# Column norms, paired output slots, a third weight buffer and a compression block of its own in a 512-token network kernel

## The chip, the cores and the metric

The kernel runs on one core of a Trainium2 chip. The metric is device time in microseconds (us), lower is better. The engines are PE (TensorE: matmuls, with PEld for its weight loads), DVE (VectorE), ACT (ScalarE), POOL (GpSimd) and SP (SyncE, which here only issues loads and stores).

## The reference

Four blocks on one sequence of 512 tokens with 1024 features, all in f32: an even mixer (spatial gating and a causal convolution) with a convolutional FFN, an odd mixer (dilated attention) with a convolutional FFN, and then two layers of a second kind.

```python
def rms_norm(x, g):
    y = xf * lax.rsqrt(jnp.mean(xf * xf, axis=-1, keepdims=True) + EPS)
    return (y * g.astype(jnp.float32)).astype(x.dtype)

def layer_norm_2(x, g, b):
    ...
    return ((xf - mu) * lax.rsqrt(var + LN_EPS)).astype(x.dtype) * g + b

def conv_ffn(x, norm_g, w_up, conv_w, conv_b, w_down):
    h = rms_norm(x, norm_g)
    u = causal_dwconv(h @ w_up, conv_w, conv_b)
    gate, val = jnp.split(u, 2, axis=-1)
    return x + (jax.nn.silu(gate) * val) @ w_down

# first_block: for each of two layers
            x = x + jnp.concatenate([ya, yb], axis=-1) @ even_w_out[j]   # or x + o @ odd_w_o[j]
        x = conv_ffn(x, ...)
    return rms_norm(x, final_norm_g)

# second_block: for each of two layers
    proj = h @ w_in[l]
    mixed = jnp.concatenate([nsa_mixer(...), gla_mixer(...), pool_mixer(...)], axis=-1)
    h = layer_norm_2(DEEPNORM_ALPHA * h + mixed @ w_out[l], ln1_g[l], ln1_b[l])
    ff = jnp.square(jax.nn.relu(h @ w_up[l])) @ w_down[l]
    h = layer_norm_2(DEEPNORM_ALPHA * h + ff, ln2_g[l], ln2_b[l])

# inside nsa_mixer, for keys and for values
        hid = jax.nn.gelu(tb.reshape(B, G, n_cmp, CMP_BLOCK * Dh) @ w1)
        return hid @ w2
```

Each norm needs, for every token, one or two sums over 1024 features, and its result is the input of the next product.

## The kernel before

Activations lie with features on the 128 partitions and the 512 tokens along them, in DC = 8 chunks of 128 features (`X`, `HH`, `HL`). All weights come as one stream of 376 slots of 128 x 1024 (512 KB each). SP loads slot s into `RAW[:, s % 2]`; ACT rounds it into `WH` (`split_hi`), DVE makes the remainder `WL` (`split_lo`), and a product is three passes, WH x HH, WH x HL and WL x HH, so one slot is 24 matmuls of 512 columns. There are two buffers, so `split_hi` of slot s waits until the matmuls of slot s-2 are over (`tile_done`), and the load into RAW waits for the `split_lo` of slot s-2.

A slot is used in one of two ways. `project` makes one output tile of 128 features from all eight chunks of the input. `add_rows` takes one chunk of the input and adds to all eight output chunks, in eight PSUM banks; on the last slot of such a product it reports each output chunk (`y_done`), and DVE's `add_out` adds it to X and reports `x_ready`. The first tile after a norm (`first_tiles`) goes chunk by chunk behind ACT and DVE, which make HH (`h_hi`) and HL (`h_lo`).

There are seven RMS norms (named even, v, conv, f0, odd, f1, final; v and conv are halves with a mean of their own) and four layer norms (ln1_0, ln2_0, ln1_1, ln2_1, the last of which ends the program). In every one, the sum over features is a matmul of a 128 x 128 matrix of ones with a chunk of squares (`sum_squares`, L1118, or `sum_rows`, L1109, for the mean), which leaves the sum in all 128 partitions. ACT takes the root of a full 128 x 512 tile (`root`, L571) and DVE its reciprocal (`spread`, L1658). For f0, odd and f1 the norm is applied after the projection, so the chain root, reciprocal runs beside tile 1, and `sum_squares` is interleaved in the first tile. For `final` and the layer norms nothing of the next product can start before it. There, to spare PE, DVE adds the last chunks up first (`squares_part`, and L1979 into MU), so that PE sums five chunks and one partial sum. A layer norm then runs: sums of X (L1109, L1113), `mean` (L1639), `centre` (L1653, x8), squares on ACT (L560), their sums (L1118), root, reciprocal, rows (L1990) with HH (L816) and HL (L1994).

The NSA compression has for keys and for values one hidden product of 64 small matmuls (64 x 128 by 31 columns, alternating between the two halves of the array). `hidden` (L1375) returns a function that `project` calls after each chunk, so they stand interleaved in tiles 5 and 7 of `mix_layer`. Its weights W1 (2 MB) and four smaller arrays are loaded by POOL (L517), once a layer, when the last slot before the layer is over (`tile_done` at `L_IN[l]`). PE first reads one of them at L1349, in tile 3, behind a wait for all five.

## Time and profile before

| | |
|---|---|
| median of three runs | 2591.74 us (2590.53 to 2593.21) |
| the profiled execution | 2597.57 us, of which its span is 2595.8 us |
| PE busy | 2463.1 us, 95% of the span |
| DVE busy, ACT busy | 1417.6 us (55%), 1087.1 us (42%) |
| POOL busy | 51.7 us (2%) |
| DMA | 210.38 MB, mean 81 GB/s |

The times of the trace are those of the profiled execution, which is 5.8 us above the median. "Idle before" a row is the time in which its engine stood still ahead of it, with the engine and line that ended the wait. The granted clock is TensorE's, 1.00 being its full level of 2.4 GHz and 0.50 the lower one of 1.2 GHz. A matmul's duration counts from its start to its last result, so a run of back-to-back matmuls is better read by the distance of their starts. In the trace one f32 matmul of the program is two PE instructions, and one of fp32r is one.

### The profile page before, as it was taken

Reading aid. Unit: us, or ns where it says so; the run is one execution under the profiler, and the core shown is the slowest. Engines: PE = TensorE matmul, PEld = TensorE weight load, DVE = VectorE, ACT = ScalarE, POOL = GpSimd, SP = SyncE. Lnnn points to the kernel's source line nnn. Section 1 sums busy time; section 2 is a strip of 40 time slices with the busy share of each in tenths; the row PEclk is TensorE's granted clock in tenths of the full one; section 3 lists DMA queues with packets and bytes.
Section 4 is the critical chain, followed back from the end, with each engine's and each line's share of the span. In section 5 each row is a group of like instructions: output and inputs, shape, how many; then the busy total and the mean of one; then the engine's idle time right before and its main releaser. Section 6 shows DMA issues by size and latency. Waiting matters only on the chain.

```text
span 2595.8 us, 33416 instructions
## 1 busy us (share of the span) xinstructions
PE 2463.1 (95%) x11814; PEld 1938.8 (75%) x11814; DVE 1417.6 (55%) x2298; ACT 1087.1 (42%) x1649; POOL 51.7 (2%) x64
## 2 busy tenths in 40 slices
PE   8989999998998999999988989999989889899997
PEld 6667888877777788886766668888857666688885
DVE  5876777236763777724367664244263774532434
ACT  4534444237883544413445443223154543431322
POOL 0000000000000000000011000000000210000000
PEclk9999999999999999999999999999999989999999
DMA  4212333321222233333211113333322112233331
GB/s 170 62 45 89 95 95 95 97 88 57 65 65 68 87 97 97 94 97 113 66 49 41 43 63 97 97 97 97 97 86 66 33 33 81 65 97 97 95 97 68
DMA packets 57422, 210.38 MB, mean 81 GB/s; under 512 B 6478, under 2 KB 6880, under 8 KB 56960
## 3 DMA queue, kind: packets, MB, share of 16 engines
q1 hardware_dynamic: 56736, 204.51, 25.7%
q0 software_dynamic: 608, 4.81, 0.5%
q8 instruction: 52, 0.85, 0.1%
q14 instruction: 26, 0.21, 0.0%
HBM read 207.20 MB, written 2.10 MB: 81 GB/s over the span
## 4 chain that ended last, share of the span: by engine, by line
PE 82%; DVE 8%; ACT 7%; issue 2%; DVEq 1%; DMA 0%; SPq 0%; ACTq 0%
PE PS L1081 14%; PE PS L1083 14%; PE PS L1082 14%; PE PS L1097 10%; PE PS L1099 10%; PE PS L1098 10%; PE PS L1118 2%; ACT PT L720 1%; PE PS L1256 1%; ACT RT L732 1%; ACT PB L714 1%; DVE RSTD L1658 1%; DVE PB L1886 1%; DVE WL L1635 1%; PE PS L1109 1%
## 5 line engine op out<-in xcount | busy, mean ns | idle before, releaser
L1635 DVE TENSOR_TENSOR WL<-RAW,WH 128x1024 fp32r<-128x1024 f32 x376 | 462.4, 1230 | 650.4 <-ACT WH L555 649.8
L555 ACT ACTIVATE WH<-RAW 128x1024 fp32r<-128x1024 f32 x376 | 397.5, 1057 | 819.4 <-PE PS L1099 560.9
L1081 PE MATMUL PS<-HH,WH 128*128 128x512 f32 x1792 | 713.3, 398 | 2.0 <-DVE WL L1635 1.9
L1083 PE MATMUL PS<-HH,WL 128*128 128x512 f32 x1792 | 699.6, 390 | 0.0
L1082 PE MATMUL PS<-HL,WH 128*128 128x512 f32 x1792 | 699.4, 390 | 0.0
L1081 PEld LDWEIGHTS PS<-HH,WH 128*128 128x128 f32 x1792 | 338.0, 189 | 77.8 <-issue 6.9
L1083 PEld LDWEIGHTS PS<-HH,WL 128*128 128x128 f32 x1792 | 337.4, 188 | 71.3
L1082 PEld LDWEIGHTS PS<-HL,WH 128*128 128x128 f32 x1792 | 338.0, 189 | 70.4 <-issue 3.4
L1099 PE MATMUL PS<-MH,WL 128*128 (+1 forms) x864 | 336.1, 389 | 0.0
L1097 PE MATMUL PS<-MH,WH 128*128 (+1 forms) x864 | 336.1, 389 | 0.0
L1098 PE MATMUL PS<-ML,WH 128*128 (+1 forms) x864 | 336.1, 389 | 0.0
L1097 PEld LDWEIGHTS PS<-MH,WH 128*128 128x128 f32 x864 | 162.2, 188 | 33.7
L1098 PEld LDWEIGHTS PS<-ML,WH 128*128 128x128 f32 x864 | 162.2, 188 | 33.6
L1099 PEld LDWEIGHTS PS<-MH,WL 128*128 128x128 f32 x864 | 162.2, 188 | 33.6
L1818 DVE SCALAR_TENSOR_TENSOR NBF<-NBF,VEC 128x511 f32<-128x511 f32 (+1 forms) x176 | 131.6, 748 | 14.1 <-issue 13.5
L2274 DVE TENSOR_TENSOR SB<-RB 128x512 f32<-128x512 f32 x64 | 44.3, 692 | 166.9 <-ACT RB L1055 166.9
L1055 ACT ACTIVATE RB<-PS 128x512 f32<-128x512 f32 x64 | 38.3, 598 | 209.4 <-PE PS L1083 203.2
L714 ACT ACTIVATE PB<-PB,NEGMAX 128x512 f32<-128x512 f32 (+3 forms) x160 | 87.7, 550 | 44.0 <-DVE NEGMAX L1873 44.0
L1811 DVE TENSOR_TENSOR NBF<-PS,RSTD 128x512 f32<-128x512 f32 x88 | 60.9, 692 | 80.1 <-PE PS L1083 79.9
L1134 PE MATMUL PS<-HH,WH 128*128 128x512 f32 x96 | 51.1, 532 | 37.6 <-DVE HL L1994 21.0
L1097 PE MATMUL PS<-HH,WH 128*128 128x512 f32 x192 | 76.6, 399 | 3.1 <-DVE HL L2182 3.1
L1873 DVE CUSTOM_DVE_ANT_0 PB<-PS,TAB 128x512 f32<-128x512 f32 (+3 forms) x160 | 68.5, 486 | 19.3 <-issue 19.3
(273 smaller groups left out, 2568.6 us busy)
## 6 DMA issues: line engine op xcount, KB each, us to landing
RAW<-wstream SPq DMA_DIRECT2D x376, 512.0 KB, 3.6
W<-cmp_w POOLq DMA_DIRECT2D x2, 2048.0 KB, 8.8
X<-xt SPq DMA_DIRECT2D x4, 512.0 KB, 6.8
out<-X SPq DMA_DIRECT2D x8, 256.0 KB, 2.0
TAB<-tables SPq DMA_DIRECT2D x1, 1871.5 KB, 12.9
WS<-spatial_w SPq DMA_DIRECT2D x1, 512.0 KB, 8.7
BS<-spatial_b SPq DMA_DIRECT2D x1, 256.0 KB, 9.2
PW<-pool_w POOLq DMA_DIRECT2D x2, 128.0 KB, 2.4
```

The lines of the kernel that those rows point to most:

```text
L555: act.activation(WH[:, b, :], RAW[:, b, :], ACT.Copy).then_inc(w_hi, 1)
L714: act.activation(row, row, ACT.Exp, scale=-1.0, bias=NEGMAX[:, 4 * e + i:4 * e + i + 1], accum_out=SUM[:, 4 * e + i:4 * e + i + 1]).then_i ...
L1081: pe.matmul(PS[:, bank, :], WH[:, b, w], HH[:, k, :], start=(k == 0), stop=False)
L1082: pe.matmul(PS[:, bank, :], WH[:, b, w], HL[:, k, :], start=False, stop=False)
L1083: last = pe.matmul(PS[:, bank, :], WL[:, b, w], HH[:, k, :], start=False, stop=(k == DC - 1))
L1097: pe.matmul(PS[:, n, :], WH[:, b, w], rh, start=first, stop=False)
L1098: pe.matmul(PS[:, n, :], WH[:, b, w], rl, start=False, stop=False)
L1099: last = pe.matmul(PS[:, n, :], WL[:, b, w], rh, start=False, stop=final)
L1635: dve.tensor_tensor(WL[:, b, :], RAW[:, b, :], WH[:, b, :].bitcast(F32), ALU.subtract).then_inc(w_lo, 1)
L1811: dve.tensor_tensor(ZF[:, b, :], PS[:, b, :], RSTD[:], ALU.mult).then_inc(f_z, 1)
L1818: ins = dve.scalar_tensor_tensor(acc, ZF[:, b, 0:T - back], w[:, 2 - back:3 - back], acc, ALU.mult, ALU.add)
L1873: dve.tensor_tensor_reduce(PB[:, e, row], head_banks(e)[:, row], tab(mask)[:, T - w:T], 1.0, 3.0e38, ALU.add, ALU.min, NEGMAX[:, 4 * e + i ...
```

## The change

It has six parts.

1. **Pairs.** Ahead of each of the eight norms that follow an `add_rows` product (f0, odd, f1, final, and the four layer norms) the last two slots are taken together (`add_pair`): output chunk by output chunk, six matmuls each, instead of one slot after the other. It waits for the `w_lo` of both slots. For `final` and the layer norms the sums of output chunk n-3 (`LAG`) stand inside the pair, behind chunk n.
2. **Column sums.** `sum_tokens` takes the data as the 128 x 128 weights and a single column of ones as the moving side, four matmuls a chunk (one per 128 tokens), which leaves the 512 sums as a 128 x 4 block, tokens on partitions. Root and reciprocal work on [128, 4]. `widen` brings them back to 128 x 512: four matmuls with the column spread over 128 columns as weights and the identity as the moving side, into a PSUM bank. DVE reads that bank directly, or, for even, f0, odd and f1, copies it to RSTD first (`keep_rstd`). The layer norm's mean goes the same way, so it has two widens. DVE's partial sums are gone. Only conv keeps the old form.
3. **Third weight buffer.** The slot of the next first tile is split into `WX` (`early_hi`, `early_lo`), which is free throughout the last slots before the norm. `first_tiles` runs WH x HH, WL x HH and only then waits for `h_lo` for WH x HL.
4. **Compression block.** `hidden` is a block of 64 matmuls of its own behind tile 5 and tile 7.
5. **POOL's loads** wait for `L_IN[l] + 1` finished slots, that is, also for the first tile of the layer.
6. **Smaller things.** The squares of f0, f1 and final have a buffer SQF of their own. In f0 `fill_scaled` writes HH rows 6 and 7, which E_OUT's pair reads, only when the pair is over. In odd the root stands behind `raw_k` on ACT as before, but the PE's widen, inside tile 1, now waits for it.

```diff
             def squares(buf, src, order, ready, base):
...
-                act.activation(STD[:], PS[:, bank, :], ACT.Sqrt, scale=1.0 / width, bias=eps).then_inc(n_std, 1)
+                if nm == "conv":
+                    act.activation(STD[:], PS[:, bank, :], ACT.Sqrt, scale=1.0 / width, bias=eps).then_inc(n_std, 1)
+                else:
+                    act.activation(COL[:, COL_STD:COL_STD + TT], PS[:, bank, 0:TT], ACT.Sqrt, scale=1.0 / width, bias=eps)\
+                       .then_inc(n_std, 1)
...
-                pool.wait_ge(tile_done, L_IN[l])
+                pool.wait_ge(tile_done, L_IN[l] + 1)
...
+            def early_hi(s):
+
+                act.wait_ge(w_loaded[0], 16 * (s // 2 + 1))
+                if s:
+                    act.wait_ge(tile_done, s - 2)
+                act.activation(WX[:, 0, :], RAW[:, 0, :], ACT.Copy).then_inc(w_hi, 1)
...
                 pe.wait_ge(w_lo, 2 * i + c + 1)
                 for k in range(DC):
+                    if beside and k == beside[0]:
+                        widen(*beside[1:])
...
-                    if beside:
-                        beside(k)
...
+            def add_pair(i, rows, beside=None):
+
+                pe.wait_ge(w_lo, 2 * i + 2)
+                for n in range(DC):
+                    w = slice(n * P, (n + 1) * P)
+                    for b, (rh, rl) in enumerate(rows):
+                        pe.matmul(PS[:, n, :], WH[:, b, w], rh, start=False, stop=False)
+                        pe.matmul(PS[:, n, :], WH[:, b, w], rl, start=False, stop=False)
+                        last = pe.matmul(PS[:, n, :], WL[:, b, w], rh, start=False, stop=(b == 1))
+                        if n == DC - 1:
+                            last.then_inc(tile_done, 1)
+                        elif b:
+                            last.then_inc(y_done, 1)
+                    if beside and n >= LAG:
+                        beside(n - LAG)
...
+            def sum_tokens(buf, n, bank, final):
+
+                for t in range(TT):
+                    last = pe.matmul(PS[:, bank, t:t + 1], buf[:, n, t * P:(t + 1) * P], tab("ones")[:, 0:1],
+                                     start=(n == 0 and t == 0), stop=(final and t == TT - 1))
+                return last
+
+            def widen(nm, col, bank):
+
+                pe.wait_ge(n_col, WIDE[nm])
+                for t in range(TT):
+                    last = pe.matmul(PS[:, bank, t * P:(t + 1) * P], COL[:, col + t:col + t + 1].to_broadcast([P, P]),
+                                     tab("identity"), start=True, stop=True)
+                last.then_inc(n_wide, 1)
...
-                        pe.wait_ge(h_lo, fill + k + 1)
-                        pe.matmul(PS[:, b, :], WH[:, b, w], HH[:, k, :], start=(k == 0), stop=False)
-                        pe.matmul(PS[:, b, :], WH[:, b, w], HL[:, k, :], start=False, stop=False)
-                        last = pe.matmul(PS[:, b, :], WL[:, b, w], HH[:, k, :], start=False, stop=(k == DC - 1))
+                        wh, wl = first_weights(b, w)
+                        pe.wait_ge(h_hi, fill + k + 1)
+                        pe.matmul(PS[:, b, :], wh, HH[:, k, :], start=(k == 0), stop=False)
+                        pe.matmul(PS[:, b, :], wl, HH[:, k, :], start=False, stop=False)
+                        pe.wait_ge(h_lo, fill + k + 1)
+                        last = pe.matmul(PS[:, b, :], wh, HL[:, k, :], start=False, stop=(k == DC - 1))
...
-            project(base, 1)
+            project(base, 1, beside=(1, "odd", COL_RSTD, 3))
...
             def layer_norm(nm):
-                sum_rows(X, 0, [(n, x_ready, XR[nm] + n + 1) for n in range(FIRST)], n_add, (n_part, PART[nm] + 1))
-                for n in range(FIRST):
-                    sum_squares(NB2, n, 3, nm, False)
-                sum_squares(NB2, FIRST, 3, nm, True, (n_part, PART[nm] + 2))
+                for n in range(DC - LAG, DC):
+                    last = sum_ready(nm, n)
+                last.then_inc(n_add, 1)
+                widen("mean_" + nm, COL_MEAN, 1)
+                for n in range(DC):
+                    sum_squares(NB2, n, 2, nm, n == DC - 1)
+                widen(nm, COL_RSTD, 3)
...
-                tile(5, hidden(0))
+                tile(5)
+                hidden(0)
...
             split_lo(base, 1)
+            inverse_root("odd")
             split_lo(base, 2)
-            spread("odd")
+            keep_rstd("odd")
```

On PE, around the first layer norm (ln1_0), the program of before has, from the last three matmuls of the product to the first of the next tile (X is the residual, NB2 the squares, TAB holds the ones):

```order
L1097 MATMUL PS<-HH,WH 128x512
L1098 MATMUL PS<-HL,WH 128x512
L1099 MATMUL PS<-HH,WL 128x512
L1109 MATMUL PS<-X,TAB 128x512 [waits x_ready] x5
L1113 MATMUL PS<-MU,TAB 128x512 [waits n_part]
L1118 MATMUL PS<-NB2,TAB 128x512 [waits n_sq] x5
L1118 MATMUL PS<-NB2,TAB 128x512 [waits n_part]
L1134 MATMUL PS<-HH,WH 128x512 [waits h_lo,w_lo]
```

The same place after the change, from the fifth token sum inside the pair on; the last two sums of X and seven of the eight chunks of squares, which read like their neighbours, are left out, and COL is the 128 x 4 block:

```order
L1144 MATMUL PS<-HH,WH 128x512
L1145 MATMUL PS<-HL,WH 128x512
L1146 MATMUL PS<-HH,WL 128x512
L1165 MATMUL PS<-TAB,X 128x1 [waits x_ready]
L1165 MATMUL PS<-TAB,X 128x1 x3
...
L1173 MATMUL PS<-TAB,COL 128x128 [waits n_col]
L1173 MATMUL PS<-TAB,COL 128x128 x3
L1165 MATMUL PS<-TAB,NB2 128x1 [waits n_sq]
L1165 MATMUL PS<-TAB,NB2 128x1 x3
...
L1203 MATMUL PS<-HH,WX 128x512 [waits h_hi,w_lo]
```

Five of eight sums of X moved ahead of the product's end; six matmuls of the squares became thirty-two of one column; two groups of four are new, each behind a wait for DVE.

On DVE, at the same norm, before:

```order
L1689 SCALAR_TENSOR_TENSOR X<-X,PS 128x512 [waits tile_done]
L1979 TENSOR_TENSOR MU<-X 128x512 [waits x_ready]
L1979 TENSOR_TENSOR MU<-MU,X 128x512 [waits x_ready]
L1635 TENSOR_TENSOR WL<-RAW,WH 128x1024 [waits w_hi]
L1639 TENSOR_SCALAR MU<-PS 128x512 [waits n_add]
L1653 TENSOR_TENSOR X<-X,MU 128x512 x8
L1646 TENSOR_TENSOR NB2<-NB2 128x512 [waits n_sq] x2
L1658 RECIPROCAL RSTD<-STD 128x512 [waits n_std]
L1990 SCALAR_TENSOR_TENSOR NB2<-X,VEC,RSTD 128x512 x2
```

and after (L1721 and L1635 are the same `split_lo`, L1777 and L1689 the same addition, L2082 and L1990 the same row):

```order
L1777 SCALAR_TENSOR_TENSOR X<-X,PS 128x512 [waits tile_done]
L2072 TENSOR_SCALAR COL<-PS 128x4 [waits n_add]
L1721 TENSOR_TENSOR WL<-RAW,WH 128x1024 [waits w_hi]
L1735 TENSOR_TENSOR X<-X,PS 128x512 [waits n_wide]
L1735 TENSOR_TENSOR X<-X,PS 128x512 x7
L1740 RECIPROCAL COL<-COL 128x4 [waits n_std]
L2082 SCALAR_TENSOR_TENSOR NB2<-X,VEC,PS 128x512 [waits n_wide]
L2082 SCALAR_TENSOR_TENSOR NB2<-X,VEC,PS 128x512
```

Four full-width additions are gone, the mean and the reciprocal shrank from 128 x 512 to 128 x 4, and `split_lo` moved behind the mean.

On PE, in tile 5 of `mix_layer` (TB the keys' blocks, W1 the compression weights), before, one chunk of eight:

```order
L1375 MATMUL PS<-TB,W1 64x31 x8
L1081 MATMUL PS<-HH,WH 128x512
L1082 MATMUL PS<-HL,WH 128x512
L1083 MATMUL PS<-HH,WL 128x512
L1375 MATMUL PS<-TB,W1 64x31 x8
```

and after, from the end of tile 5 to the start of tile 6:

```order
L1117 MATMUL PS<-HH,WH 128x512
L1118 MATMUL PS<-HL,WH 128x512
L1119 MATMUL PS<-HH,WL 128x512
L1453 MATMUL PS<-TB,W1 64x31 [waits c_tb]
L1453 MATMUL PS<-TB,W1 64x31 x63
L1117 MATMUL PS<-HH,WH 128x512 [waits w_lo,z_kept]
```

The eight groups of eight stand in one row.

## Rows read from the trace of the kernel before

**Rows 1.** The page, part 1: busy time, share of the span, instructions of each engine.
```profile
PE 2463.1 (95%) x11814; PEld 1938.8 (75%) x11814; DVE 1417.6 (55%) x2298; ACT 1087.1 (42%) x1649; POOL 51.7 (2%) x64
```

**Rows 2.** The page, part 4: the chain that ended last, by engine.
```profile
PE 82%; DVE 8%; ACT 7%; issue 2%; DVEq 1%; DMA 0%; SPq 0%; ACTq 0%
```

**Rows 3.** Timeline, last two slots ahead of ln1_0: start, us, what.
```profile
1504.53 0.39 PE L1097 MATMUL PS<-HH,WH 128*128 128x512 f32 x1
1504.76 0.39 PE L1098 MATMUL PS<-HL,WH 128*128 128x512 f32 x1
...
1505.88 1.23 DVE L1635 TENSOR_TENSOR WL<-RAW,WH 128x1024 fp32r<-128x1024 f32 x1 [4.21 <-ACT WH L555]
```

**Rows 4.** Timeline, ln1_0 from the product's end to the first tile.
```profile
1515.42 4.46 PE L1109 MATMUL PS<-X,TAB 128*128 128x512 f32 x10
...
1518.05 0.20 ACT L565 ACTIVATE WARM<-TAB 128x1 f32<-128x1 f32 x1
...
1521.54 4.91 DVE L1653 TENSOR_TENSOR X<-X,MU 128x512 f32<-128x512 f32 x8
...
1522.94 4.56 PE L1118 MATMUL PS<-NB,TAB 128*128 128x512 f32 x10 [2.21 <-ACT NB L560]
...
1529.94 3.35 DVE L1658 RECIPROCAL RSTD<-STD 128x512 f32<-128x512 f32 x1 [1.94 <-ACT STD L571]
1533.38 1.42 DVE L1990 SCALAR_TENSOR_TENSOR NB<-X,VEC,RSTD 128x512 f32<-128x512 f32 x2
...
1535.82 0.77 PE L1134 MATMUL PS<-HH,WH 128*128 128x512 f32 x1 [6.64 <-DVE HL L1994]
```

**Rows 5.** Timeline: matmuls with 128 x 128 weights and 31 moving columns.
```profile
1293.83 0.31 PE L1392 MATMUL PS<-HID,W 128*128 128x31 f32 x2
1294.07 0.40 PE L1393 MATMUL PS<-W,HID 128*31 128x128 f32 x2
```

**Rows 6.** Timeline: matmuls with 64-row weights, alternating between the array's halves.
```profile
1359.11 1.08 PE L1401 MATMUL PS<-KCS,ZT 64*128 64x31 f32 x16
1361.82 0.80 PE L1424 MATMUL PS<-ZS 64*128 64x512 f32 x2 [1.62 <-DVE ZT L2132]
```

**Rows 7.** Windows: stretch, length, busy time of PE, PEld, DVE, ACT, POOL, then granted clock.
```profile
1520.70:1522.90 2.20, 0.03 (x1) 0.00 (x0) 2.06 (x4) 0.64 (x2) 0.00 (x0) 1.00 0.68 223
...
1532.20:1535.80 3.60, 0.00 (x0) 0.01 (x1) 3.38 (x5) 1.63 (x3) 0.00 (x0) 0.50 0.00 0
...
1361.00:1364.00 3.00, 2.18 (x10) 1.82 (x11) 2.16 (x6) 0.41 (x1) 1.64 (x3) 0.57 0.00 0
```

**Rows 8.** Waits by line: us in total, times, longest (tile 2 behind even, f0, f1).
```profile
PE PS L1081 <- DVE WL L1635: 1.9, 3, 0.7
```

**Rows 9.** Timeline, odd: the keys' copies on ACT and the first scores on PE.
```profile
598.29 0.63 ACT L756 ACTIVATE KS<-KR 64x512 fp32r<-64x512 f32 x1 [0.61 <-DVE KR L1897]
...
604.13 1.54 PE L1272 MATMUL PS<-KL,QS 64*128 64x512 f32 x8 [5.14 <-DVE QS L1909]
```

**Rows 10.** Timeline, final: sums of squares and the first tile.
```profile
1212.02 5.31 PE L1118 MATMUL PS<-NBF,TAB 128*128 128x512 f32 x12
...
1223.82 0.76 PE L1134 MATMUL PS<-HH,WH 128*128 128x512 f32 x1 [6.48 <-DVE HL L1672]
```

**Rows 11.** Timeline, tile 5 of layer 0: two of the eight interleaved groups.
```profile
1259.29 0.65 PE L1375 MATMUL PS<-TB,W 64*64 64x31 f32 x16
...
1260.77 0.65 PE L1375 MATMUL PS<-TB,W 64*64 64x31 f32 x16
```

**Rows 12.** The page, part 6: POOL's 2 MB load, KB each, us to landing.
```profile
W<-cmp_w POOLq DMA_DIRECT2D x2, 2048.0 KB, 8.8
```

**Rows 13.** Timeline, layer 0: POOL's first and last load, PE's first use.
```profile
1212.85 0.75 POOL L517 DMA_DIRECT2D GW<-gate_w  x1 [1196.91 <-PE PS L1099]
...
1215.20 0.54 POOL L517 DMA_DIRECT2D W<-cmp_w  x1
...
1243.09 1.56 PE L1349 MATMUL PS<-GW,ZT 17*128 17x192 f32 x8
```

242 lines of the change are left out of this document (142 added, 100 removed).

## The prediction

> **What bounds the kernel now.** I read the busy times first, then the chain that ended last, then the timeline around each norm. PE is busy for 95% of the span [rows 1] and carries 82% of the chain [rows 2]: a plain slot is 24 matmuls 0.226 us apart [rows 3], 5.44 us, and all else hides beside it. What is left for other engines, 15% for DVE and ACT [rows 2], lies where PE has nothing to multiply. At a layer norm that is the stretch from the product's end at 1515.42 to the first tile at 1535.82, 20.40 us [rows 4], of which PE sums for 4.46, then 4.56, and waits 2.21 and 6.64 us, with the 3.35 us reciprocal as the longest single step. So the norms are worth attacking; the question is what the replacement costs on PE, which is the bound. All sums are against the profiled execution (2597.57 us, 5.8 above the median); I add them to the median.
>
> **The pair's wait.** `add_pair` waits for both slots' weights. The second one's split can't begin before slot s-3 is over, since there are two buffers. The trace has this order of events: the slot starts at 1504.53, ACT rounds, DVE's remainder starts at 1505.88 and ends 1.23 later, at 1507.11 [rows 3]. Before, that was hidden by the slot then running. Now nothing else is ready: PE stands for 1507.11 - 1504.53 = 2.6 us, at eight places. Behind it on PE is only the pair; but everything after it shifts. It buys little: the output chunks appear 1.36 us apart instead of 0.68, so DVE's adds no longer fall behind and the sums of the early chunks can be made inside, yet the last chunk comes at the same end. WX lets the next slot's split go on meanwhile, off the path.
>
> **The price of one token sum.** One chunk was one f32 matmul of 512 columns: ten PE instructions take 4.46, so 0.86 us for two [rows 4]. It becomes four matmuls, eight instructions, each with its own 128 x 128 weights and one moving column. No such instruction is in the trace. From above: two instructions with 128 x 128 weights and 31 columns take 0.24 us up to the next line [rows 5], 0.12 each with the change of line. From below: sixteen with 64-row weights, alternating between the halves of the array, take 1.08 to the last result; a lone one lasts 0.20 (0.31 less 0.11, [rows 5]), so they start (1.08 - 0.20) / 15 = 0.06 apart [rows 6]. I take 0.11, because the token sums fill all 128 rows with one weight block after another, as in rows 5. Then a chunk costs 8 x 0.11 = 0.88, no less than before; between other matmuls I count 1.0, for the changes of kind. The narrow side doesn't pay: it saves columns, and the loads of weights take their place. The loads themselves overlap in rows 6 since halves alternate. A rule of the Trainium skill fits this (page "TensorE: Matmul & The Clock Gate", section "The mechanism": a weight load overlaps running matmuls only when its row group differs), and the two rows agree with it, 0.11 against 0.06. Another rule of the same page speaks for less (section "Back-to-back issue gap": matmuls of 1 to 64 columns at about 60 cycles, or an issue floor near 25 ns); by it the kernel would come out faster, near the second rival's time.
>
> **A layer norm, step by step** (ln1_0, in the times of before). Pair over, with five token groups inside: 1515.42 + 2.6 + 5 x 1.0 = 1523.0. Three groups left: 1525.6. Mean on [128, 4], priced like the 0.20 us ACT step on one column [rows 4]: 1525.9. Then DVE makes `split_lo`, 1.23, which hides the 0.9 us widen: centring starts at 1527.1, against 1521.54 [rows 4], 5.6 later. Before, it was the other way: that split ran under the sums. The first square is there 1.4 after centring starts (1522.94 - 1521.54 [rows 4]): 1528.5. Eight groups on PE, 7.0, are slower than ACT's squares (0.6 each), so 1535.5. Root and reciprocal 0.2 each with 0.25 of hand-over: 1536.15. Widen with its hand-over 1.0: rows at 1537.15, against 1533.38 [rows 4]: 3.8 later. So the reciprocal's 3.2 us are won, and 2.6 of waiting, two widens and unshared sums cost more. The first tile gets back 0.4, as one matmul instead of three stands behind the last HL. Per norm 3.4, and 3.8 for the last, which has no tile: **+14.0** with TensorE at its full clock.
>
> **The clock.** From the end of the pair (1523.0) to the first tile (some 1539) PE has nothing but one-column sums and a widen. The rows show the following: after 2.2 us of no work the clock is still 1.00 [rows 7]; after the sums of squares end and PE stands, it is 0.50 from 1532.2 on [rows 7]. And at 1359.11 sixteen narrow matmuls run, then PE is idle for 1.62 us only [rows 6], and still the clock falls in that stretch (0.57 on the mean of 1361 to 1364 [rows 7]). Had narrow matmuls held the clock up, an idle time shorter than 2.2 should not have lowered it. So I take it that one-column sums don't count as work and the squares run at the lower level, 1.2 GHz. At half rate the eight groups cost another 7.0 and the widen 0.9: +7.9 each, **+31.6** for four. The wait inside the pair (2.6) is near the 2.2 that didn't lower it; up to 0.9 at each of eight, counted for the range alone.
>
> **The RMS norms.** f0 and f1: 2.6 for the pair, 1.0 for the widen inside tile 1; root and reciprocal are ready by then. Sums cost as before. The idle 0.6 or so ahead of tile 2 [rows 8] goes, because the 3.35 reciprocal no longer holds up DVE's split: +3.0 each. even: the widen 1.0, less that idle 0.7, and 1.0 for v's, less 0.2 of sums: +1.1. In v the reciprocal was hidden by tap matmuls. odd: 2.6; PE's widen waits about 3 us in tile 1, since the root stands behind `raw_k` on ACT, but PE has 5.14 idle later [rows 9], waiting for the scores' operands. Tile 1 ends later, ACT's work on the queries too, and its copies of the keys start 1.1 after the 598.29 of before [rows 9]; less 0.4 in the first tile: +3.3. final: 1212.02 [rows 10] + 2.6 + 5.0 + 2.6 for sums, 0.65, 1.0: rows at 1223.9 against 1221.5 (2.3 ahead of the first tile, as in rows 4 and 10); less 0.4: +1.9. Its first tile was at half clock and stays so. Together **+12.3**.
>
> **POOL's loads.** Issued after tile 0 instead of before it: 1212.85 before [rows 13]; tile 0 starts at 1223.82 [rows 10] and, part of it at half clock, ends near 1233.9. The 2 MB load is the fifth on the queue, 2.35 behind the first [rows 13], and takes 8.8 [rows 12]: 1233.9 + 0.3 + 2.35 + 8.8 = 1245.4, against 1243.09 for the first use [rows 13]. RAW's 512 KB loads share the engines now: 2.3 to 3.4 late, 3.0 taken, twice: **+6.0**. Before, it was over long in advance.
>
> **The compression block.** Two groups are 1.48 us apart [rows 11], of which 3 x 0.226 = 0.68 is the tile's: 0.80 a group, 6.4 for eight. Sixteen start (0.65 - 0.20) / 15 = 0.03 apart [rows 11]; 128 in a row take 4.0 with both ends. That is 2.35 saved, four times: **-9.4**. ACT and DVE are not late there, so it goes through in full.
>
> **Sum.** 14.0 + 31.6 + 12.3 + 6.0 - 9.4 = +54.5: 2591.74 + 54.5 = 2646.2; with a little for the waits' clock, 2648.
>
> **Rival 1, the clock holds.** Same prices, but one-column sums (which do keep PE's queue and its weight loads busy) count as work: 54.5 - 31.6 = +22.9, 2614.6; with the waits' clock up to 2620. For it: through the interleaved narrow groups of rows 11 the clock stays up. Against: full matmuls stand between those.
>
> **Rival 2, the other side: the token sums are cheap.** If a block of weights goes in while the other one is in use, as in rows 6, an instruction is 0.06, a chunk 0.5 alone and 0.62 in between. A layer norm then has its mean at 1515.42 + 2.6 + 3.1 + 1.5 + 0.2 = 1522.8, centres at 1524.1 to 1524.5, its sums keep pace with ACT's squares, and the rows start at 1532.2: 1.1 earlier, and 0.4 of the first tile, -5.8 for four. The RMS norms come to +0.8 instead of 12.3, loads and block stay: -8.4, **2583.3**. It decides at the price per instruction: between 0.11 (+22.9) and 0.06 (-8.4) zero lies near 0.075. With the clock down in the squares it is a gain of 1 or nothing.
>
> **Rival 3: pairs or loads don't cost what I say.** If POOL's loads are in time, -6; the pairs' waits are structural, and without them alone all would be 21 less. Neither changes the sign of the forecast; they sit in the range.
>
> **How the numbers follow.** Forecast (full weight loads, low clock) 0.57, 2640 to 2662. Rival 1 0.26, 2608 to 2622. Rival 2 0.17: 2583 in 0.11, no change in 0.06. The likeliest gives 2648. Leaving out rival 2 leaves out 0.17, so the range is 2608 to 2662. Slower 0.83, within 0.2% (5 us, about what a measurement of this kernel can tell from no change) 0.06, faster 0.11.
>
> **What would show it.** In the profile after: an idle of 2.6 us ahead of each pair, ended by DVE's WL; token instructions 0.11 apart at full clock and 0.22 in the squares of the layer norms, with a granted clock of 0.50 there; 18 us from centring to rows of a layer norm (10 with the clock up) where 11.8 were [rows 4]; at L1349's counterpart an idle of 3 us ended by POOL's load; 4.0 us for the compression block. Wrong if the instructions stand 0.06 apart, or the clock stays at 1.00 through the squares.

## The result and the profile after

The changed kernel takes 2673.3 us (median of four runs, 2665.98 to 2685.01) against 2592.47 for the kernel before: 1.0317 times as long, interval 1.0281 to 1.0353, or 81 us more. The forecast was slower, 2648, with a range to 2662. The direction was right, the size was not. One run of the small-loads kernel below took 3231.33 us at a mean granted clock of 0.734 and is left out of that kernel's median. The profiled run of after is one of the two faster ones, 2665.98 us with a span of 2664.2; against the profiled run of before it is 68.4 longer.

The page of after, parts 1 and 4, to be read beside [rows 1, 2]. PE is busier by 71 us, although it does no more full matmuls, and the token sums (L1165) are the largest new line of the chain.

```profile
PE 2534.0 (95%) x12610; PEld 2058.9 (77%) x12610; DVE 1377.4 (52%) x2284; ACT 1083.0 (41%) x1649; POOL 51.8 (2%) x64
...
PE 83%; DVE 7%; ACT 6%; issue 2%; DMA 1%; DVEq 1%; POOL 0%; SPq 0%; ACTq 0%; POOLq 0%
```

The waits of PE in after: total us, times, longest. The first and the last of these lines don't exist in before; they are the pairs and POOL's loads.

```profile
PE PS L1144 <- DVE WL L1721: 20.4, 8, 2.6
...
PE PS L1429 <- DMA W<-cmp_w: 6.4, 2, 3.5
```

The timeline of after at ln1_0, which answers to [rows 3, 4] (L1144 is the pair, L1165 a token sum, L1173 a widen, L1735 centring, L2082 the row, L1203 the first tile):

```profile
1527.40 0.47 PE L1144 MATMUL PS<-HH,WH 128*128 128x512 f32 x1 [2.56 <-DVE WL L1721]
...
1543.66 3.63 PE L1165 MATMUL PS<-TAB,X 128*128 128x1 f32 x32
...
1547.54 1.16 PE L1173 MATMUL PS<-TAB,COL 128*128 128x128 f32 x8 [0.25 <-DVE COL L2072]
1548.74 4.87 DVE L1735 TENSOR_TENSOR X<-X,PS 128x512 f32<-128x512 f32 x8
...
1550.14 13.81 PE L1165 MATMUL PS<-TAB,NB 128*128 128x1 f32 x64 [1.44 <-ACT NB L579]
1563.99 0.26 ACT L593 ACTIVATE COL<-PS,TAB 128x4 f32<-128x4 f32 x1 [9.72 <-PE PS L1165]
1564.29 0.18 DVE L1740 RECIPROCAL COL<-COL 128x4 f32<-128x4 f32 x1 [10.68 <-ACT COL L593]
1564.52 2.08 PE L1173 MATMUL PS<-TAB,COL 128*128 128x128 f32 x8 [0.57 <-DVE COL L1740]
1566.63 1.40 DVE L2082 SCALAR_TENSOR_TENSOR NB<-X,VEC,PS 128x512 f32<-128x512 f32 x2 [2.17 <-PE PS L1173]
...
1568.28 0.76 PE L1203 MATMUL PS<-HH,WX 128*128 128x512 f32 x1 [1.68 <-ACT HH L843]
```

The wait stands ahead of the pair as predicted. Thirty-two token instructions take 3.63 us, 0.11 each; sixty-four take 13.81, 0.22 each. From centring to the first row it is 17.9 us, where before had 11.8 and the prediction said 18. The reciprocal has shrunk from 3.35 to 0.18. The windows of after around the same norm (length, busy times, then the granted clock):

```profile
1528.50:1532.00 3.50, 3.50 (x10) 2.70 (x9) 0.86 (x2) 0.00 (x0) 0.00 (x0) 0.52 0.81 274
1532.00:1546.00 14.00, 14.00 (x90) 12.50 (x88) 4.63 (x7) 2.06 (x2) 0.00 (x0) 1.00 0.01 4
...
1549.50:1568.00 18.50, 15.89 (x72) 15.51 (x72) 5.65 (x10) 5.62 (x10) 0.00 (x0) 0.50 0.09 29
```

The lowest line is the forecast's stretch at half clock. The highest was not in the sum: 1.2 us after the pair's wait of 2.56 the clock falls to half for some 3.4 us, in the middle of full matmuls. Such a stretch stands at six of the eight pairs, all but those of f0 and ln2_1; it begins between 0.3 us before PE resumes (ln2_0) and 1.2 us after it (ln1_0).

Where the 68.4 us of the two profiled runs lie, by the start of the same slots in both:

| stretch | forecast | measured |
|---|---|---|
| even block, into E_OUT | +1.1 | +2.2 |
| f0: pair, first tile, tile 1 | +3.0 | +4.2 |
| odd: the same | +3.3 | +4.2 |
| odd attention | 0 | +2.5 |
| f1: pair, first tile, tile 1 | +3.0 | +7.3 |
| final: pair to first tile | +1.9 | +3.7 |
| mixer of layer 0, of layer 1 (loads, block) | -1.7, -1.7 | -3.9, -1.6 |
| ln1_0, ln2_0, ln1_1 | +11.3 each | +12.6, +13.2, +12.7 |
| ln2_1, to the end | +11.7 | +11.4 |
| sum | +54.5 | +68.4 |

At each of the eight pairs PE starts 2.7 us later than it would without the wait, 2.6 of waiting and 0.1 of restart.

The lower clock can be added up in the same way. In the profiled run of before TensorE is at half level for 105 us of the span, in that of after for 211. Of the 106 us more, 82 lie in the four layer norms, counted from the pair to the end of the first tile or tiles, and 24 in all other places together. Where PE is busy throughout, a microsecond at half level costs half a microsecond.

### The profile page after: what moved, and what is told of

Its sections match the earlier page's. It is cut to its first block, busy times and chain, and to the rows that moved or that the text cites. A ratio compares the mean times of both kernels' runs of the same rounds, so it can differ in the third digit from the quotient of the medians.

```text
span 2664.2 us, 34958 instructions
## 1 busy us (share of the span) xinstructions
PE 2534.0 (95%) x12610; PEld 2058.9 (77%) x12610; DVE 1377.4 (52%) x2284; ACT 1083.0 (41%) x1649; POOL 51.8 (2%) x64
## 4 chain that ended last, share of the span: by engine, by line
PE 83%; DVE 7%; ACT 6%; issue 2%; DMA 1%; DVEq 1%; POOL 0%; SPq 0%; ACTq 0%; POOLq 0%
PE PS L1117 13%; PE PS L1119 13%; PE PS L1118 13%; PE PS L1131 8%; PE PS L1133 8%; PE PS L1132 8%; PE PS L1165 4%; PE PS L1144 1%; ACT PB L740 1%; PE PS L1328 1%; ACT RT L758 1%; ACT PT L746 1%; PE PS L1146 1%; PE PS L1145 1%; DVE WL L1721 1%
## 5 line engine op out<-in xcount | busy, mean ns | idle before, releaser
L1721 DVE TENSOR_TENSOR WL<-RAW,WH 128x1024 fp32r<-128x1024 f32 x368 | 452.5, 1230 | 608.0 <-ACT WH L567 607.6
L1117 PE MATMUL PS<-HH,WH 128*128 128x512 f32 x1792 | 710.4, 396 | 0.0
L1131 PE MATMUL PS<-MH,WH 128*128 (+1 forms) x800 | 311.2, 389 | 0.0
L1132 PE MATMUL PS<-ML,WH 128*128 (+1 forms) x800 | 311.2, 389 | 0.0
L1133 PE MATMUL PS<-MH,WL 128*128 (+1 forms) x800 | 311.2, 389 | 0.0
L1131 PEld LDWEIGHTS PS<-MH,WH 128*128 128x128 f32 x800 | 150.2, 188 | 31.3
L1133 PEld LDWEIGHTS PS<-MH,WL 128*128 128x128 f32 x800 | 150.2, 188 | 31.1
L1132 PEld LDWEIGHTS PS<-ML,WH 128*128 128x128 f32 x800 | 150.2, 188 | 31.1
L702 ACT ACTIVATE NBF<-NBF,VEC 128x512 f32<-128x512 f32 x88 | 70.4, 800 | 6.8 <-DVE NBF L1906 6.8
L1165 PEld LDWEIGHTS PS<-TAB,NB 128*128 128x128 f32 x352 | 67.2, 295 | 7.4 <-ACT NB L579 6.6
## 6 DMA issues: line engine op xcount, KB each, us to landing
TAB<-tables SPq DMA_DIRECT2D x1, 1871.5 KB, 13.2
```

Source lines behind the costliest of these rows:

```text
L702: act.activation(ACCS[:, b, :], ZF[:, b, :], ACT.Identity, scale=w[:, 2:3], bias=w[:, 3:4]).then_inc(f_acc, 1)
L1117: pe.matmul(PS[:, bank, :], WH[:, b, w], HH[:, k, :], start=(k == 0), stop=False)
L1131: pe.matmul(PS[:, n, :], WH[:, b, w], rh, start=first, stop=False)
L1132: pe.matmul(PS[:, n, :], WH[:, b, w], rl, start=False, stop=False)
L1133: last = pe.matmul(PS[:, n, :], WL[:, b, w], rh, start=False, stop=final)
L1165: last = pe.matmul(PS[:, bank, t:t + 1], buf[:, n, t * P:(t + 1) * P], tab("ones")[:, 0:1], start=(n == 0 and t == 0), stop=(final and t = ...
```

## The experiments

Every run has the kernel before beside it on the same chip, at 2593.0 to 2595.2 us.

### The compression block alone

```diff
-                tile(5, hidden(0))
+                tile(5)
+                hidden(0)
```
(and the same for tile 7, on the kernel before)

> The kernel before with one edit, the compression block: the hidden products stand as one block behind tiles 5 and 7 instead of interleaved in them. Theory: 128 instructions start 0.03 us apart in a row and the 0.3 us per group for the changes of kind goes, 2.35 us at each of four places: -9.4, 2583 us. Rival (the interleaved matmuls cost nothing, since they wait on the same weights and PE is held by ACT and DVE in those tiles): 0, 2592 us.

Measured: 2584.87 us, ratio 0.9966 (0.9954 to 0.9977): -8.3. The theory holds. By slots, each tile behind a block starts 2.3 earlier, relative to the kernel before, as forecast (2.35); the median shows 8.3 of the 9.4.

### The pairs undone

```diff
             def add_pair(i, rows, beside=None):

-                pe.wait_ge(w_lo, 2 * i + 2)
-                for n in range(DC):
-                    w = slice(n * P, (n + 1) * P)
-                    for b, (rh, rl) in enumerate(rows):
+                for b, (rh, rl) in enumerate(rows):
+                    pe.wait_ge(w_lo, 2 * i + b + 1)
+                    for n in range(DC):
+                        w = slice(n * P, (n + 1) * P)
...
-                    if beside and n >= LAG:
-                        beside(n - LAG)
+                        if b and beside and n >= LAG:
+                            beside(n - LAG)
```

> The changed kernel with the pairs undone: the last two slots run one after the other, each behind the wait for its own weights; the sums inside stay in the last slot. Theory: the wait of 2.6 us goes at eight places (-21.8 with the restart), and with it the stretches at half clock that the trace shows 1 to 3 us behind a wait at several of them (1.7 us each): 2637 to 2650 us. Rival (the wait alone, no clock): -21.8, 2651 us. Second rival (the wait only moves to the next slot, because the sums inside then wait for DVE's additions, which come 0.68 us apart): 0 to -8, 2665 to 2673 us.

Measured: 2649.65 us (2637.81 to 2658.89), ratio to before 1.0212 (1.019 to 1.0235), 23.7 less than the changed kernel. The wait has gone from PE's list, and nothing took its place: the wait of the token sums for ACT (5.8 us in all) is the same with and without pairs. The second rival is out. Between the first two, the wait alone (-21.8) and the wait with its clock (down to -36), the median doesn't decide. The trace does. From pair to first tile, over all eight norms, this kernel's profiled run is 24.1 us shorter than after's, against 21.8 for the waits. It has no short half-clock stretch behind the start of the last two slots any more, but at ln1_0 the clock now falls earlier in the norm, during the sums of X, and the first widen pays for it as well:

```profile
1532.03 4.37 PE L1165 MATMUL PS<-TAB,X 128*128 128x1 f32 x32
1536.66 2.07 PE L1173 MATMUL PS<-TAB,COL 128*128 128x128 f32 x8 [0.26 <-DVE COL L2072]
```

```profile
1517.50:1534.60 17.10, 17.10 (x105) 15.15 (x103) 7.84 (x10) 4.30 (x4) 0.00 (x0) 1.00 0.22 67
1534.80:1562.00 27.20, 23.25 (x97) 21.46 (x98) 11.54 (x19) 9.69 (x18) 0.00 (x0) 0.50 0.06 20
```

In after these two rows are 3.63 and 1.16. The time at half level around ln1_0 is 27.3 us in both kernels (3.4 + 23.9 in after), and over all eight norms 137 us here against 139. Without the wait the norms get back the wait and little else: the first rival fits the trace best.

### The pairs' wait filled

```diff
+                for _ in range(11):
+                    pe.matmul(PS[0:128, DC - 1, :], ZERO[:], rows[0][0], start=False, stop=False)
                 pe.wait_ge(w_lo, 2 * i + 2)
```

> The changed kernel with eleven matmuls of a block of zeros, 512 columns each (2.5 us), put ahead of each pair's wait. They add zero to a bank, so nothing else changes; the wait is only filled. Theory (the idle wait lowers the clock and the pair pays for it, 1.7 us at five to eight places): -8 to -14, 2659 to 2665 us, and a granted clock of 1.00 through all pairs. Rival (a wait of 2.6 us costs only itself): 0, 2673 us.

Measured: 2665.51 us (2651.89 to 2678.55), ratio to before 1.0293 (1.0272 to 1.0314); 7.8 less than the changed kernel, with 11 more matmuls at eight places. In the trace of this run, ahead of ln1_0's pair:

```profile
1517.21 2.74 PE L1142 MATMUL PS<-HH,ZERO 128*128 128x512 f32 x11
1519.84 0.50 PE L1147 MATMUL PS<-HH,WH 128*128 128x512 f32 x1
```

and its windows over the filling and over the first part of the pair:

```profile
1517.00:1519.80 2.80, 2.80 (x13) 2.05 (x11) 1.24 (x2) 2.01 (x2) 0.00 (x0) 1.00 0.13 51
1519.80:1524.00 4.20, 4.20 (x19) 3.45 (x19) 2.50 (x3) 0.00 (x0) 0.00 (x0) 1.00 0.58 179
```

Where after has 0.52, this has 1.00, at the same place of the program and with the pair starting as late; the same holds at all eight pairs. So it is the idle time that lowers the clock there. But what this saves is small, because the clock then falls earlier in the norm behind it:

```profile
1519.80:1538.20 18.40, 18.36 (x113) 16.23 (x112) 6.63 (x9) 2.54 (x3) 0.00 (x0) 1.00 0.18 58
1538.40:1565.50 27.10, 23.39 (x93) 21.15 (x94) 13.08 (x21) 11.37 (x20) 0.00 (x0) 0.50 0.07 20
```

The eight stretches from pair to first tile are 4.5 us shorter than in after, 3.3 of it at f1 alone; the other 9.6 us between the two profiled runs lie in places that the edit doesn't touch. The medians' -7.8 is at the near end of what was expected, but the two kernels' runs overlap (2651.89 to 2678.55 against 2665.98 to 2685.01). The expected clock at the pairs is shown; the expected price of 1.7 us at each of them is not.

### Full matmuls among the token sums

```diff
             def layer_norm(nm):
...
+                busy(2)
                 widen("mean_" + nm, COL_MEAN, 1)
+                busy(8)
                 for n in range(DC):
+                    busy(2)
                     sum_squares(NB2, n, 2, nm, n == DC - 1)
```
(`busy(k)`: k matmuls of 512 columns into a free bank, on the changed kernel)

> The changed kernel with full matmuls of 512 columns, whose results nobody reads, put into the four layer norms: two ahead of the mean's widen, eight behind it and two ahead of each chunk's squares sums. They cost PE 0.45 us a chunk. Theory (one-column sums don't count as work, so the clock falls; the full ones hold it up): a chunk's sums go from 1.72 to 0.88 us at a granted clock of 1.00, so that with the filling a chunk takes 1.4 to 1.5, the widens 0.9 instead of 2.1, and the first tile runs at full clock: -3 to -4 per norm, -14 in all, 2659 us. Rival (the squares' sums cost 1.72 whatever the clock is): +3.6 for each norm's filling, +14, 2687 us.

Measured: 2688.2 us (2676.22 to 2694.05), ratio to before 1.0362 (1.034 to 1.0385), 14.9 more than the changed kernel. That is the number of the rival, but by luck: the timeline of ln1_0 in this run shows neither of the two:

```profile
1560.03 0.95 PE L1165 MATMUL PS<-TAB,NB 128*128 128x1 f32 x8
1560.84 0.72 PE L1400 MATMUL PS<-HH 128*128 128x512 f32 x2
1561.39 0.95 PE L1165 MATMUL PS<-TAB,NB 128*128 128x1 f32 x8
...
1564.13 0.98 PE L1165 MATMUL PS<-TAB,NB 128*128 128x1 f32 x8
...
1565.97 1.70 PE L1165 MATMUL PS<-TAB,NB 128*128 128x1 f32 x8
1567.53 1.20 PE L1400 MATMUL PS<-HH 128*128 128x512 f32 x2
1568.53 1.70 PE L1165 MATMUL PS<-TAB,NB 128*128 128x1 f32 x8
```

with the windows before and behind the change:

```profile
1560.00:1564.80 4.80, 4.80 (x38) 4.48 (x37) 2.82 (x5) 3.48 (x6) 0.00 (x0) 1.00 0.15 60
1565.00:1575.40 10.40, 10.35 (x41) 9.50 (x41) 0.00 (x0) 0.01 (x1) 0.00 (x0) 0.50 0.00 0
```

For four chunks the clock is 1.00 and a group of sums takes 0.95 to its last result, 1.36 to the next group with the filling in between; for the other four it is 0.50, 1.70 and 2.56. So the same instructions cost half as much when the clock is up, as the theory says, but this filling did not hold the clock up to the end of the sums. PE was busy almost without a gap in both windows. What failed was the means, not the price: every filling matmul ran at 0.42 us instead of 0.24 from then on.

### The layer norms' squares through the matrix of ones

```diff
             def sum_squares(buf, n, bank, nm, final):
...
-                if nm == "conv":
+                if nm == "conv" or nm.startswith("ln"):
                     last = pe.matmul(PS[:, bank, :], tab("ones"), buf[:, n, :], start=(n == 0), stop=final)
...
-                widen(nm, COL_RSTD, 3)
...
-                inverse_root(nm)
-                dve.wait_ge(n_wide, WIDE[nm])
+                dve.wait_ge(n_std, NORM[nm][1] + 1)
+                dve.reciprocal(RSTD[:], STD[:])
+                dve.drain()
```
(and the root and the rows on full tiles)

> The changed kernel with one thing undone in the four layer norms: the sums of squares go through the matrix of ones again, 512 columns, all eight chunks, with the root and the reciprocal on full tiles. The mean stays in columns, the pairs stay. Theory (one-column sums run at half clock, 1.72 us a chunk against 0.86 for the ones, and cost more than the narrow reciprocal saves): from the start of centring to the first row 12.8 us instead of 17.9, -5.1 at four places, -20, 2653 us; a little more if the first tile is at full clock too. Rival (at equal clock, 0.88 a chunk, the narrow form would be 2 to 3 us shorter than this one, so that undoing it costs): +8 to +12, 2681 to 2685 us.

Measured: 2659.95 us (2653.09 to 2668.03), ratio to before 1.026 (1.024 to 1.028): -13.4. The sign is the theory's, against the rival: even with the 3.35 us reciprocal back, the wide form is shorter here, at the clock that each form gets; the two at equal clock were not compared. The size is less than the 20 expected, and the timeline shows why (L1181 are the ones):

```profile
1554.63 4.87 DVE L1734 TENSOR_TENSOR X<-X,PS 128x512 f32<-128x512 f32 x8
...
1556.04 9.92 PE L1181 MATMUL PS<-NB,TAB 128*128 128x512 f32 x16 [1.44 <-ACT NB L579]
```

Sixteen instructions should take 6.9 (0.43 each, [rows 4]). They take 9.92, because the clock is already down when they start, behind the mean in columns:

```profile
1556.00:1562.00 6.00, 5.96 (x8) 2.59 (x9) 3.50 (x6) 4.16 (x7) 0.00 (x0) 0.53 0.21 81
1562.00:1566.00 4.00, 3.96 (x10) 1.45 (x8) 0.00 (x0) 0.00 (x1) 0.00 (x0) 1.00 0.00 0
```

Three us a norm, at most 12 in all: what follows a narrow stretch pays for it.

### POOL's small loads early

```diff
-                pool.wait_ge(tile_done, L_IN[l] + 1)
-                for dst, src in ((GW, gate_w), (PW, pool_w), (W2, cmp_w2), (CP, cmp_p), (W1, cmp_w1)):
+                pool.wait_ge(tile_done, L_IN[l])
+                for dst, src in ((GW, gate_w), (PW, pool_w), (W2, cmp_w2), (CP, cmp_p)):
                     pool.dma_start(dst[:], src[l]).then_inc(m_loaded, 16)
+                pool.wait_ge(tile_done, L_IN[l] + 1)
+                pool.dma_start(W1[:], cmp_w1[l]).then_inc(w1_loaded, 16)
```
(and DVE waits for `w1_loaded` ahead of the compression blocks)

> The changed kernel with the four small loads of POOL issued where they were before, at the end of the last slot before a layer, and the 2 MB load alone left behind the first tile, with a semaphore of its own that DVE waits for ahead of the compression blocks. Theory (PE's first use, which waited for all five loads, needs a small one only): the idle of 3.5 and 2.8 us in tile 3 goes, and with it the stretch at half clock that follows it in both layers (about 2 each): -6 to -10, 2663 to 2667 us. Rival (the 2 MB load is needed soon after anyway, by the compression blocks, and the wait only moves there): 0, 2673 us.

Measured: 2664.63 us (median of five, 2655.46 to 2676.33), ratio to before 1.0288 (1.0268 to 1.0308): -8.7, within the expected 6 to 10, though the runs overlap with after's. In the trace the two mixers are 4.4 and 4.6 us shorter than in after, against waits of 3.5 and 2.8. The wait is gone (L1432 is after's L1429; there it stood idle for 3.54):

```profile
1266.72 0.60 PE L1428 MATMUL PS<-TAB,ZT 128*128 128x128 f32 x4
1267.24 1.56 PE L1432 MATMUL PS<-GW,ZT 17*128 17x192 f32 x8
```

W1 can't go first as well: its memory is the third weight buffer's, which the first tile reads. That is where the later load comes from.

### Three parts undone at once, and then the mean

The first kernel of this section is the three edits above together (pairs, ones for squares, small loads). The second has in addition:

```diff
-                return sum_tokens(X, n, 0, n == DC - 1)
+                return pe.matmul(PS[:, 0, :], tab("ones"), X[:, n, :], start=(n == 0), stop=(n == DC - 1))
...
-                widen("mean_" + nm, COL_MEAN, 1)
...
+                if slot:
+                    split_lo(0, slot)
                 dve.wait_ge(n_add, ADD[nm])
-                dve.tensor_scalar(COL[:, COL_MEAN:COL_MEAN + TT], PS[:, 0, 0:TT], 1.0 / D, None, ALU.mult).then_inc(n_col, 1)
-                if slot:
-                    split_lo(0, slot)
-                dve.wait_ge(n_wide, WIDE["mean_" + nm])
-                centre(X, range(DC), PS[:, 1, :])
+                dve.tensor_scalar(MU[:], PS[:, 0, :], 1.0 / D, None, ALU.mult)
+                dve.drain()
+                centre(X, range(DC))
```

> The changed kernel with three parts undone at once: the pairs, the column sums of squares of the layer norms (ones again, as in the run for that alone) and the four small loads of POOL. What is left of the change is the column form in the other norms, the mean in columns, the third weight buffer, the order in the first tile and the compression block. Theory, parts that add up: 2673.3 less 23.7 (pairs, measured), less 20 (ones), less 6 to 10 (loads) = 2620 to 2624 us. From the kernel before upwards the steps alone give less: 2593 - 8.3 for the block, + 12 for the mean in columns (3 at each layer norm), + 4 for eight full sums instead of six, + 3 for the widens of the other norms = 2604 us. The gap between the two is what the clock costs in the narrow stretches that are left; if the clock did not matter there, the run should be near 2604.

Measured: 2632.91 us (2618.72 to 2638.59), ratio 1.0146 (1.0122 to 1.0169), 40.4 less than the changed kernel. The three alone gave 23.7 + 13.4 + 8.7 = 45.8: they add up to within the spread of the runs. It misses the 2620 to 2624 that was expected, and is 29 above the 2604 that steps at full clock would give.

> The run with three parts undone (pairs, column squares of the layer norms, small loads; 2632.9 us), and now the layer norms' mean too goes through the matrix of ones, with the full-width mean on DVE and its split ahead of it as before. What is left of the change: the column form in the RMS norms and v, the third weight buffer, the order in the first tile, the compression block, and eight full sums where two partial ones were shared with DVE. Theory (the mean in columns delays centring by 4.3 us a norm, for the token groups inside the last slot, the widen and DVE's split in between, and its narrow stretch lowers the clock, so that the ones sums behind it take 9.4 instead of 6.9): -6.7 at four places, 2606 us. Rival (only the delay, while the clock falls there in any case): -4.3 at four places, 2616 us.

Measured: 2627.04 us (2614.65 to 2631.47), ratio 1.0133 (1.0115 to 1.0151), only 5.9 less by the medians. The two profiled runs, 2629.67 and 2614.65, are 15 apart, and by slots each of the first three layer norms costs 3.6 more than in before, where it cost 6.7 with the mean in columns. So the mean in columns is 3.1 a norm in the traces; of the clock's share in it the medians say nothing certain. At ln1_0, the time at half level goes from 17.1 to 10.2 us. Neither expectation is met in its number.

What is left is mostly the RMS norms and v: by the first tile of the second half this kernel's profiled run is 12.0 behind before, with no pair in it. The terms of the sum without the pairs (even 1.1, the widens less the idle time 0.4 at f0 and f1, 0.7 at odd) gave 2.6. Its clock is at half for 6.8, 3.4 and 6.8 us in the first tiles of f0, odd and f1, where before has none, and 10.2 us longer than before in the even block. How such a stretch comes about can be read in after's timeline of f1:

```profile
871.93 3.88 PE L1165 MATMUL PS<-TAB,SQF 128*128 128x1 f32 x24
875.67 0.77 PE L1117 MATMUL PS<-HH,WH 128*128 128x512 f32 x1
...
877.10 1.91 PE L1173 MATMUL PS<-TAB,COL 128*128 128x128 f32 x8
```

```profile
874.00:880.00 6.00, 6.00 (x23) 5.51 (x24) 1.06 (x3) 1.21 (x2) 0.00 (x0) 0.50 0.00 0
```

The interleaved groups of the first tile, then three in a row, 24 instructions: the clock is at half, and all of tile 1's start and the widen (1.91 instead of 1.16) pay for it, without one idle microsecond. In after the pair's wait ends 24 us ahead of this fall; here, with no such wait, the clock falls all the same.

### The parts that help, alone

```diff
-                        pe.wait_ge(h_lo, fill + k + 1)
-                        pe.matmul(PS[:, b, :], WH[:, b, w], HH[:, k, :], start=(k == 0), stop=False)
-                        pe.matmul(PS[:, b, :], WH[:, b, w], HL[:, k, :], start=False, stop=False)
-                        last = pe.matmul(PS[:, b, :], WL[:, b, w], HH[:, k, :], start=False, stop=(k == DC - 1))
+                        pe.wait_ge(h_hi, fill + k + 1)
+                        pe.matmul(PS[:, b, :], WH[:, b, w], HH[:, k, :], start=(k == 0), stop=False)
+                        pe.matmul(PS[:, b, :], WL[:, b, w], HH[:, k, :], start=False, stop=False)
+                        pe.wait_ge(h_lo, fill + k + 1)
+                        last = pe.matmul(PS[:, b, :], WH[:, b, w], HL[:, k, :], start=False, stop=(k == DC - 1))
```
(on the kernel before, with the compression block)

> The kernel before with two parts of the change alone: the compression block, and the new order in the first tiles (WH x HH, WL x HH, then the wait for HL, WH x HL) with the weights in their two buffers as before. Theory: the block gives 8.3 as measured alone, the order 0.4 at each of eight first tiles, 3.2: 2581.5 us. Rival (the order gives nothing, because the first tile is paced by ACT and DVE at 1.3 us a chunk and its last chunk waits for the same HL): 2585 us.

Measured: 2580.11 us (2578.76 to 2584.72), ratio 0.9951 (0.9938 to 0.9964), and 2579.63 in a second set of runs. The order gives 4.8 on top of the block, a little over the 3.2 of the theory.

### The idle time ahead of the first tile filled

```diff
             def layer_norm(nm):
...
                 sum_squares(NB2, FIRST, 3, nm, True, (n_part, PART[nm] + 2))
+                if nm != f"ln2_{DEPTH2 - 1}":
+                    busy(6)
```
(and `busy(6)` at final; here `busy` is f32, the ones by the cosine table, on the version above)

> The fastest version so far (the kernel before with the block and the new order in the first tile, 2580.1 us) with six f32 matmuls of 512 columns, whose results nobody reads, in PE's idle time between a norm's last sum and its first tile: at final and at three layer norms, 5.1 us of the 6.5 idle. Theory (what lowers the clock there is the lack of full matmuls, and nothing else): the granted clock stays at 1.00 into the first tile; since that tile is paced by DVE at 1.33 us a chunk and at half clock by PE at 1.28, little is won: 0 to -1 per place, 2577 to 2580 us. Rival (the clock is lowered by something that filling doesn't reach): clock 0.50 in the first tile as before, 2580 us or a little later.

Measured: 2576.23 us (2575.67 to 2580.57), ratio 0.9942 (0.9929 to 0.9956), beside 2579.63 for the version without:

> The fastest version again, beside the run with the filled idle time, so that the two share a chip: 2580 us.

The timeline ahead of ln1_0's first tile and the windows over the filling and the tile:

```profile
1513.24 5.31 PE L1106 MATMUL PS<-TAB 128*128 128x512 f32 x12
1519.26 0.47 PE L1138 MATMUL PS<-HH,WH 128*128 128x512 f32 x1 [0.70 <-ACT HH L816]
```

```profile
1513.20:1519.20 6.00, 5.36 (x13) 2.08 (x11) 4.82 (x4) 1.50 (x3) 0.00 (x0) 1.00 0.00 0
1519.20:1524.00 4.80, 3.98 (x12) 1.82 (x12) 4.80 (x8) 4.80 (x9) 0.00 (x0) 1.00 0.00 0
```

In before the same place has 0.50 [rows 7]. Work that nobody reads keeps the clock up where wide matmuls fill the gap. At the four places themselves it gains nothing: from the last two slots to the first tile, ln1_0 and ln1_1 take 30.50 us with the filling and 30.49 without, final 21.96 and 21.95, and ln2_0 31.38 and 30.49. The first tile takes as long at either clock, as the expectation had it. The 3.6 us between the two profiled runs lie elsewhere, mostly in the mixer of layer 0, which is 4.4 us shorter in this run. Its windows, with the filling and without:

```profile
1223.00:1484.00 261.00, 239.37 (x1642) 184.55 (x1642) 153.97 (x373) 130.74 (x232) 21.27 (x22) 0.99 0.18 53
1223.00:1488.00 265.00, 243.63 (x1641) 186.36 (x1640) 154.18 (x374) 130.49 (x231) 21.25 (x22) 0.97 0.17 52
```

In the run of the same program without filling that was profiled earlier this mixer took 3.0 us more still, so whether the filling causes the difference is not shown. By the median this is the fastest version, 3.4 us under the one without and 17 under the kernel before.

## Why the prediction was wrong in size

**What bounds the kernel** held: PE's queue and, at the norms, the chain behind it.

**The clock** is the step that failed. The sum has it for the stretch from the mean to the first tile of the four layer norms alone, +31.6, which is 63 us at half level, and has "up to 0.9 at each of eight" behind the pairs' waits for the range, and nothing for the RMS norms, the even block and the attention. The profiled run of after is at half level for 106 us more than before, of which 82 are in the layer norms and 24 elsewhere. The reason given for leaving the pairs out was that 2.2 us of idle had not lowered the clock [rows 7], a row 0.4 us shorter than the case; 2.6 us did, at six of eight.

What these stretches cost is a different matter. Counted where they stand, six times 1.7 us is 10. But with the wait undone or filled, the stretches behind it are gone and the norms are only 2.3 and 4.5 us shorter beyond the wait, with 137 and 132 us at half level against 139. In both runs most of the half-level time that stood behind the pair now stands in the narrow groups that follow. So the runs put the lost time down to the narrow groups more than to the wait.

**The pair's wait** itself held: eight waits of 2.56, 20.4 us in all, against 8 x 2.6.

**The price of a token sum** held: 3.63 us for 32, 0.11 each, between the bounds 0.06 and 0.12, and the groups between other matmuls take 0.9 where 1.0 was said. The rule of the Trainium skill that a weight load overlaps running matmuls only when its row group differs (page "TensorE: Matmul & The Clock Gate", section "The mechanism") fits it: 0.11 us with full-height blocks of weights, against 0.06 with alternating halves [rows 6]. The table for narrow matmuls (the same page, "Back-to-back issue gap"), which gives about 60 cycles or 25 ns for 1 to 64 columns, would not have priced it: 0.11 us is over four times that. The section itself calls these gaps those of isolated matmuls and says that in a stream of weight loads and matmuls both set the spacing, and each token instruction brings its own weights. The second rival is out.

**A layer norm and its clock** held nearly: 11.3 forecast, 12.6 to 13.2 measured, and 11.7 against 11.4 for the last, 4.3 too little over the four. At ln1_0 the fall behind the pair adds 1.7 us that the forecast doesn't have; groups cheaper than the counted 1.0 give some of it back. The squares run at 0.50, 0.22 an instruction. Rival 1, the clock holds, is out.

**The RMS norms** were mis-sized, +12.3 forecast against 21.6 measured (the first, second, third, fifth and sixth stretch of the table). These stretches have 24 us more at half level than in before, which can cost up to 12 of PE's time and so covers the 9 missing. The prediction looked for the clock only where PE has nothing but narrow work for 15 us. It also falls where narrow groups stand among wide ones and then three in a row, as at f1, and the wide matmuls behind pay. The kernel without pairs has as much half-level time in these five stretches. The odd attention adds 2.5 that the forecast had at nothing, with 7 us more at half level.

**POOL's loads** held: 6.4 us of waiting against 6.0; the small ones issued early, -8.7. **The block** held: -9.4 forecast, -8.3 measured alone.

**The run that was profiled** hides the rest. The sum of all terms by slots is 68.4, 14 above the forecast's 54.5; the medians are 81 apart. The granted clock of the four runs is 0.960, 0.955, 0.957 and 0.962 with 2665.98, 2680.6, 2685.01 and 2665.99 us. A mean clock lower by 0.005 is 27 us more at half level, which costs up to 13 us. So the two slower runs are those with more time at half level; for the slowest, 0.003 explains some 8 of 19 us. How far this varies can be seen in the even block: up to slot 20 after and all kernels made from it by undoing or filling run the same matmuls, and their profiled runs are there 1.4 to 6.7 us behind before, with 13.7 to 23.9 us at half level against 10.2. The kernel before has a spread of 4 to 7 us in its sets of runs, the changed one of 19. The prediction gave a range for prices and none for this.

Open: how much of the RMS norms' excess is the first tile's interleaved groups and how much the widen, the share of the clock in the mean, where the 12 us lie by which the median is above the profiled run, and why the clock falls in one run and not in the next at the same place. Each experiment has one trace, and the kernels with narrow sums spread by 15 to 27 us, so the small differences of their medians (-7.8, -8.7, -5.9) are not certain one by one.

## What to carry to other kernels

A matmul with one moving column costs the load of its weights: replacing 512 columns by four 128 x 128 weight blocks saves PE nothing (0.88 against 0.86 us). In this kernel the granted clock went to 0.50 in and behind such stretches, which the wide matmuls behind them then pay for. Before a wait goes on the path of the bounding engine, count its length: here removing it gave back 24.1 us for 21.8 of waiting. A lower clock seen behind an idle time is not yet its price: fill or remove the idle time and look at where the clock falls then. Parts of a change that are bundled should be priced alone: here two small ones were worth 13 us, and the rest lost 94. And before a gain is put down to an edit, look whether it lies at the edit's place.

## What the runs showed of the hardware

- Uninterrupted PE work isn't enough for the full clock: with token sums and two 512-column matmuls in turn (1.36 us a turn at first, PE busy almost throughout) the clock was at 1.00 for four turns and at 0.50 for the next four.
- After an idle time of 2.2 us at the four layer norms of before the clock stayed at 1.00. Around an idle time of 2.56 us in after it fell at six of eight places; with full matmuls of zeros in the same gap it fell at none.
- The fall isn't tied to one moment of the idle time: in after it came 0.3 us before PE resumed at ln2_0 and 1.2 us after PE had resumed full work at ln1_0.
- Taking away one cause of the fall need not save time at half level: around ln1_0 it was 27.3 us with the pair's wait, without it, and with it filled.
- A tile that is paced by another engine can lose nothing to the lower clock: the first two tiles behind ln1_0 took 13.89 us with the clock held at 1.00 and 13.89 with 3.4 us of them at half level.
- Kernels can differ in spread: four runs took 2665.98 to 2685.01 us with more narrow stretches, against 2590.53 to 2594.21.
